# The first two weight blocks fetched in quarters, inputs and norm weights in order of need, and the sum of squares one chunk later

## The reference

```
x = x + 0.5 * swiglu(rms_norm(x, g1), w_gate, w_up, w_down)      # FFN, hidden width 2816
x = x + mixer(rms_norm(x, g2))                                   # attention and pooling
x = x + 0.5 * swiglu(rms_norm(x, g3), ...)
... # the second block: FFN, gated mixer, FFN, and a last rms_norm

def rms_norm(x, g):
    return x * rsqrt(mean(x * x, axis=-1) + 1e-6) * g
def swiglu(x, w_gate, w_up, w_down):
    return (silu(x @ w_gate) * (x @ w_up)) @ w_down
```

## Time and profile before

| | us |
|---|---|
| median of 3 runs | 1095.96 (1095.06 to 1097.74) |
| the profiled execution, its own time | 1094.97 |
| its span, from the first to the last instruction | 1093.2 |
| TensorE busy | 1080.8 (99% of the span) |
| VectorE busy | 783.8 (72%) |
| ScalarE busy | 617.4 (56%) |
| GpSimd busy | 187.8 (17%) |

### The profile page before, as it was taken

How to read it: one execution, slowest core, us unless ns; L and a number is a source line. 1 busy time by engine, 2 the same in 40 slices (tenths; PEclk the granted TensorE clock), 3 DMA queues, 4 the chain that set the end, 5 groups by cost and what they waited for, 6 DMA issues and landing times.

```text
span 1093.2 us, 17873 instructions
## 1 busy us (share of the span) xinstructions
PE 1080.8 (99%) x6282; PEld 944.2 (86%) x6282; DVE 783.8 (72%) x1114; ACT 617.4 (56%) x945; POOL 187.8 (17%) x199
## 2 busy tenths in 40 slices
PE   8999999999999999999999999999999999999997
PEld 6888888888988888888888888889988898888886
DVE  6866666797797666668666676787877669666664
ACT  7655544465675555456555545755655557555541
POOL 4411101020031111011111100133201012111100
PEclk9999999999999999999999999999999999999998
DMA  7755555453256555556555554655455545655561
GB/s 280 269 188 189 186 180 175 171 177 134 96 175 210 192 190 176 191 175 209 195 188 188 182 191 155 221 183 192 155 192 182 185 152 203 201 191 190 177 192 39
DMA packets 55571, 200.02 MB, mean 183 GB/s; under 512 B 6304, under 2 KB 6304, under 8 KB 55392
## 3 DMA queue, kind: packets, MB, share of 16 engines
q1 hardware_dynamic: 54576, 196.11, 52.9%
q0 software_dynamic: 512, 2.65, 0.6%
q10 hardware_dynamic: 432, 0.57, 0.2%
HBM read 198.26 MB, written 1.05 MB: 182 GB/s over the span
## 4 chain that ended last, share of the span: by engine, by line
PE 94%; DVE 4%; DMA 1%; ACT 0%; issue 0%; ACTq 0%; DVEq 0%
PE pair L1256 53%; PE pair L1257 27%; PE pair L1250 4%; PE pair L1252 4%; PE pair L1251 4%; DVE w_lo L780 1%; DVE x_hl L786 1%; PE pair L1472 1%; DMA x<-x_in 1%; PE pair L1482 0%; DVE x L797 0%; PE pair L1535 0%; PE pair L1577 0%; PE pair L1493 0%; DVE x_sq L926 0%
## 5 line engine op out<-in xcount | busy, mean ns | idle before, releaser
L780 DVE TENSOR_TENSOR w_lo<-w_raw,w_hi 128x1024 fp32r<-128x1024 f32 x369 | 462.1, 1259 | 226.3 <-ACT w_hi L429 225.9
L1256 PE MATMUL pair<-x_hl,w_hi 128*128 128x512 f32 x1728 | 606.6, 396 | 2.6 <-DVE x_hl L786 1.6
L429 ACT ACTIVATE w_hi<-w_raw 128x1024 fp32r<-128x1024 f32 x369 | 386.4, 1056 | 240.5 <-PE pair L1257 205.2
L1257 PE MATMUL pair<-x_hl,w_lo 128*128 128x256 f32 x1728 | 483.5, 280 | 0.0
L1256 PEld LDWEIGHTS pair<-x_hl,w_hi 128*128 128x128 f32 x1728 | 323.9, 187 | 80.5 <-DVE w_lo L780 2.0
L1257 PEld LDWEIGHTS pair<-x_hl,w_lo 128*128 128x128 f32 x1728 | 326.1, 189 | 0.1
L1256 PE MATMUL pair<-wide,w_hi 128*128 128x512 f32 x832 | 291.0, 394 | 0.0
L1257 PE MATMUL pair<-wide,w_lo 128*128 128x256 f32 x832 | 232.7, 280 | 0.0
L1256 PEld LDWEIGHTS pair<-wide,w_hi 128*128 128x128 f32 x832 | 156.0, 187 | 36.4
L1257 PEld LDWEIGHTS pair<-wide,w_lo 128*128 128x128 f32 x832 | 157.0, 189 | 0.0
L347 POOL TENSOR_TENSOR wide<-side,wide 128x256 fp32r<-128x256 f32 x88 | 86.5, 983 | 375.9 <-ACT wide L491 375.9
(11 more groups left out here) (185 smaller groups left out, 829.2 us busy)
## 6 DMA issues: line engine op xcount, KB each, us to landing
w_raw<-stream SPq DMA_DIRECT2D x369, 512.0 KB, 4.2
const<-const_in POOLq DMA_DIRECT2D x1, 1248.0 KB, 8.3
w_raw<-stream SPq DMA_DIRECT2D x4, 256.0 KB, 5.7
out<-x_sq SPq DMA_DIRECT2D x4, 256.0 KB, 2.6
rows<-rows_in POOLq DMA_DIRECT2D x1, 576.0 KB, 10.3
x<-x_in ACTq DMA_DIRECT2D x2, 256.0 KB, 5.7
x<-x_in SPq DMA_DIRECT2D x2, 256.0 KB, 7.0
sgu_w<-sgu_w_in POOLq DMA_DIRECT2D x1, 512.0 KB, 13.3
```

Source lines behind the costliest of these rows:

```text
L429: nc.scalar.activation(w_hi[:, slot, :], w_raw[:, slot, :], ACT.Copy).then_inc(w_hi_done, 1)
L780: nc.vector.tensor_tensor(w_lo[:, slot, :], w_raw[:, slot, :], w_hi[:, slot, :].bitcast(F32), ALU.subtract).then_inc(w_split, 1)
L1256: nc.tensor.matmul(dst, a_hi, b_hl.rearrange("p a s -> p (a s)"), start=first, stop=False, skip_group_check=True)
L1257: return nc.tensor.matmul(dst[:, 0:S], a_lo, b_hl[:, 0, :], start=False, stop=last, skip_group_check=True)
```

## The change

The left halves of blocks 0 and 1 become two quarters each, with transfers, copies, subtractions and waits of their own. Tile 0 and tile 1 of x become transfers of their own, with `cols` between them, and tiles 4 and 5 move from SP's queue to ACT's. On ACT, all squares move behind the split of block 2: tiles 0 to 3 ahead of the split of block 3, tiles 4 to 7 behind it. On TensorE the sum of squares of the first FFN moves from ahead of chunk 2 (blocks 4 and 5) to behind it; on ACT and DVE the splits of blocks 8 and 9 move from between the first steps of the FFN to ahead of the root and of its inverse. There are 12 warming matmuls in place of 16.

```diff
         @block.sync
-            for n in range(2):
-                sp.dma_start(w_raw[:, n, 0:HALF], stream[n, :, 0:HALF]).then_inc(half_arrived[n], 16)
+            for q in range(2):
+                for n in range(2):
+                    part = slice(q * QUARTER, (q + 1) * QUARTER)
+                    sp.dma_start(w_raw[:, n, part], stream[n, :, part]).then_inc(quarter_arrived[2 * q + n], 16)
             for n in range(2):
                 sp.dma_start(w_raw[:, n, HALF:BW], stream[n, :, HALF:BW]).then_inc(arrived[n], 16)
-            for c in range(2, 4):
-                sp.dma_start(x[:, 2 * c:2 * c + 2, :], x_in[:, 2 * c:2 * c + 2, :]).then_inc(x_loaded[c], 16)
+            sp.dma_start(x[:, 6:8, :], x_in[:, 6:8, :]).then_inc(x_loaded[2], 16)
...
+            def first_quarter(q):
+                for n in range(2):
+                    part = slice(q * QUARTER, (q + 1) * QUARTER)
+                    act.wait_ge(quarter_arrived[2 * q + n], 16)
+                    nc.scalar.activation(w_hi[:, n, part], w_raw[:, n, part], ACT.Copy).then_inc(quarter_hi_done, 1)
+
             def first_input():
-                for c in range(4):
-                    act.wait_ge(x_loaded[c], 16)
-                    input_hi(0, 2 * c)
-                    input_hi(0, 2 * c + 1)
-                    if c == 1:
-                        for n in range(2):
-                            act.wait_ge(arrived[n], 16)
-                            nc.scalar.activation(w_hi[:, n, HALF:BW], w_raw[:, n, HALF:BW], ACT.Copy).then_inc(w_hi_done, 1)
-                    if 1 <= c < 3:
-                        square(0, 2 * c - 2)
-                        square(0, 2 * c - 1)
+                first_quarter(0)
+                act.wait_ge(cols_loaded, 16)
+                for k in range(2):
+                    act.wait_ge(x_first[k], 16)
+                    input_hi(0, k)
+                first_quarter(1)
+                act.wait_ge(x_loaded[0], 16)
+                for k in range(2, 4):
+                    input_hi(0, k)
+                for n in range(2):
+                    act.wait_ge(arrived[n], 16)
+                    nc.scalar.activation(w_hi[:, n, HALF:BW], w_raw[:, n, HALF:BW], ACT.Copy).then_inc(w_hi_done, 1)
+                for c in range(2, 4):
+                    act.wait_ge(x_loaded[c - 1], 16)
+                    for k in range(2 * c, 2 * c + 2):
+                        input_hi(0, k)
                 split(2)
+                for k in range(4):
+                    square(0, k)
+                split(3)
                 for k in range(4, KC):
                     square(0, k)
...
             def ffn(e, n0, p):
-                for b in range(3, 8):
+                for b in range(3 if p else 4, 8 if p else 10):
                     split(n0 + b)
                 rms_root(p)
...
                 fetch(0, 2)
-                split(n0 + 8)
+                if p:
+                    split(n0 + 8)
                 gate(0)
                 fetch(1, 3)
                 hidden(0)
-                split(n0 + 9)
+                if p:
+                    split(n0 + 9)
                 gate(1)
...
-            act.dma_start(x[:, 0:2, :], x_in[:, 0:2, :]).then_inc(x_loaded[0], 16)
+            act.dma_start(x[:, 0, :], x_in[:, 0, :]).then_inc(x_first[0], 16)
             act.dma_start(cols[:], cols_in).then_inc(cols_loaded, 16)
-            act.dma_start(x[:, 2:4, :], x_in[:, 2:4, :]).then_inc(x_loaded[1], 16)
+            act.dma_start(x[:, 1, :], x_in[:, 1, :]).then_inc(x_first[1], 16)
+            act.dma_start(x[:, 2:4, :], x_in[:, 2:4, :]).then_inc(x_loaded[0], 16)
+            act.dma_start(x[:, 4:6, :], x_in[:, 4:6, :]).then_inc(x_loaded[1], 16)
...
         @block.vector
...
-                for b in range(3, 7):
+                for b in range(3, 7 if p else 9):
                     split(n0 + b)
                 mean_square(p)
-                split(n0 + 7)
+                split(n0 + (7 if p else 9))
                 inverse_root(p)
...
         @block.tensor
...
             def ffn(e, n0, p):
-                if p == 0:
-                    pe.wait_ge(half_split, 2)
                 for k in range(KC):
+                    if p == 0 and k in (0, 2):
+                        pe.wait_ge(quarter_split, k + 2)
...
-                sum_squares(p)
+                if p:
+                    sum_squares(p)
...
                     chunk(f, (f + 2) % 4)
+                    if p == 0 and f == 2:
+                        sum_squares(p)
...
-WARM = 16
+WARM = 12
```

More of the change, by code:

```diff
@@ L45 @@
 BW = 1024
-HALF = BW // 2
+HALF, QUARTER = BW // 2, BW // 4
 RING = 4
@@ L181, in build @@
         arrived = [sem(f"arrived{i}") for i in range(RING)]
-        half_arrived = [sem(f"half_arrived{i}") for i in range(2)]
-        half_hi_done = sem("half_hi_done")
-        half_split = sem("half_split")
+        quarter_arrived = [sem(f"quarter_arrived{i}") for i in range(4)]
+        quarter_hi_done = sem("quarter_hi_done")
+        quarter_split = sem("quarter_split")
         w_hi_done = sem("w_hi_done")
@@ L187, in build @@
         w_used = sem("w_used")
-        x_loaded = [sem(f"x_loaded{c}") for c in range(4)]
+        x_first = [sem(f"x_first{k}") for k in range(2)]
+        x_loaded = [sem(f"x_loaded{c}") for c in range(1, 4)]
         cols_loaded = sem("cols_loaded")
@@ L1208, in gated_mixer @@
                 residual(p)
[L1210 to L1215, removed]
+            for q in range(2):
+                for n in range(2):
+                    part = slice(q * QUARTER, (q + 1) * QUARTER)
+                    dve.wait_ge(quarter_hi_done, 2 * q + n + 1)
+                    nc.vector.tensor_tensor(w_lo[:, n, part], w_raw[:, n, part], w_hi[:, n, part].bitcast(F32),
+                                            ALU.subtract).then_inc(quarter_split, 1)
+                for k in range(2 * q, 2 * q + 2):
+                    input_lo(0, k)
             for n in range(2):
```

## The result

The changed kernel is slower: median 1098.6 us of 22 runs (1095.26 to 1103.12), against 1094.57 us for the kernel before in 22 runs of the same series. The two medians are 4.0 us apart; the ratio formed from all the runs is 1.0046 [1.0035, 1.0057], or 5.0 us. Its profiled execution took 1100.22 us with a span of 1098.4 us, 5.2 us more than the execution of the earlier trace rows.

What follows compares the result with a forecast made beforehand. TensorE's unbroken stream bounds the kernel. Block 2's 1.2 us gain is spent on the late sum and root, and GpSimd's 1.6 us delay less 0.75 us spare makes +0.9 us: 1096.9 us, range 1093.8 to 1099.4 us.

Steps and rivals of the forecast that it cites:

- The wait at block 8: TensorE waits briefly at block 8 for the first add, due 6.95 us behind block 5's end; block 8 0.9 us late.
- Step 1: Front of TensorE's stream: with squares moved, ACT copies block 2 sooner and block 2 starts at 14.2 us, 1.2 us earlier.
- Step 2: GpSimd's queue: the seven additions start at about 13.6 us, take 8.2 us again and end at 21.8 us, 1.6 us later.
- rival E: Port lock between VectorE and GpSimd: additions take 10.0 us, block 11 starts 2.7 us later; 1098.7 us, chance 0.05.
- Step 3: Block 11 on TensorE: late hidden_lo delays DVE's subtraction, so block 11 starts at 42.27 us, 0.9 us later than before.
- the clock as a rival: At the start: twelve warming matmuls may end before the clock rises, leaving early blocks at 1.2 GHz; block 11 3.2 us later.
- the prediction's last sign of being wrong: On TensorE: the prediction is wrong if a matmul pair takes 0.64 us after 8 us.
- A: A gain arrives: block 2 gains 1.5 us, only the 0.8 us stall is lost; 0.7 us faster, 1095.3 us, chance 0.25.
- B: Small transfers are slow: block 2 gains only 0.5 us, block 11 starts 1.6 to 2.3 us later; 1098 us, chance 0.10.
- D: First sum of squares stalls TensorE beyond 0.8 us because DVE is still at block 8; 1097.5 to 1098 us, chance 0.04.
- slower: Outcome that the measurement tells the changed kernel from no change, 0.3% (3.3 us), on the slow side; chance 0.06.
- C: Clock still at 1.2 GHz for blocks 0 and 1 after fewer warming matmuls: 3.2 us later, 1099.2 us, chance 0.06.

Runs made afterwards that it cites:

- experiment 1: Changed kernel with GpSimd's tables moved behind hidden_lo(0) in its queue: median 1096.69 us, ratio 1.0029.
- experiment 3: Changed kernel with the last four of GpSimd's seven additions of squares 8 columns wide instead of 256: median 1096.83 us, ratio 1.0031.
- experiment 5: Kernel before with only the squares moved, tiles 0 to 3 behind block 2's split, 4 to 7 behind block 3's: 1099.05 us, ratio 1.004.
- experiment 6: Changed kernel with the sum of squares and the splits of blocks 8 and 9 back at their old places: 1099.01 us, ratio 1.0043.
- experiment 12: Changed kernel, unchanged, profiled a second time: one time of 1099.37 us, no interval.
- experiment 8: Changed kernel with the squares alone back between the inputs, the sum of squares still one chunk later: 1100.13 us, ratio 1.0062.
- experiment 10: Changed kernel with the squares back between the inputs and the split of block 9 behind the inverse root: 1096.89 us, ratio 1.002.
- experiment 7: Kernel before with only the quarters, the input order and 12 warming matmuls: 1094.46 us, ratio 1.0011.
- experiment 4: Changed kernel with ten matmuls on zeros ahead of block 11, to fill the pause: median 1098.77 us, ratio 1.0052.
- experiment 9: Changed kernel with GpSimd's tables behind hidden_lo(0) and the split of block 9 behind the inverse root: 1095.7 us, ratio 1.0019.
- experiment 11: Kernel before, unchanged, profiled a second time: one time of 1092.0 us, no interval.
- experiment 2: Kernel before with GpSimd's tables moved behind hidden_lo(0): 1094.76 us, ratio 1.0001.

## Why the prediction was wrong

**What held.** The places were right: a wait with `ms` (0.65 against 0.8 us), one at block 10, one at block 11 released by DVE's subtraction, with DVE behind `hidden_lo`. With E, the end of block 5, at 26.50 us, the first `add` ended at E + 6.94, where 6.95 had been worked out, block 10 came at E + 13.3 (13.1), and the time from the last addition to `hidden_lo` was 17.4 us (17.6 before). The wait at block 8 did not come: the 6.95 us were met, but so was block 8's place, moved by the wait with `ms`. From 52 us on there is no difference.

**Step 1, "block 2 1.2 us earlier": 0.2 us.** The sentence that failed is that the 5.66 us of blocks 0 and 1 "fit in front of block 2 either way, if their last tiles come by 12.8 us". Tiles 4 to 7 are 8 pairs, 2.83 us; for block 2 at 14.2 us tile 4 has to start by 11.4 us. It started at 12.30, released by DVE's input half, because ACT's inputs of tiles 4 to 7 stood behind the right half of block 1, which landed at 10.4 us. TensorE's own tile 4 had run at about the same time before; when I took away ACT's squares, that became what set block 2. DVE had block 2's split ready at 14.84 us.

**Step 2, GpSimd's queue, +1.6 us: +4.65 us.** It is two terms. The additions began at 14.27 instead of 13.6 us, since ACT's copy of block 2 was at 12.53 and not 11.8. And they took 10.6 us, not the 8.2 carried over from before. That size was the worst error, and rival E (10.0 us, 0.05) had it nearly right. The additions one by one, start to end in us, worked out from the trace:

```
before  11.00-11.72 12.10-13.00 13.14-13.88 14.46-15.94 16.08-16.81 16.96-18.49 18.63-20.17
after   14.27-15.44 15.59-16.33 16.47-18.00 18.15-19.80 19.94-21.47 21.62-23.15 23.29-24.82
```

Alone an addition takes 0.74 us, beside a subtraction of DVE 1.53 us. Before, four of seven ran beside nothing or nearly so; behind the splits of blocks 2 and 3 DVE always has a subtraction at hand, and only one was that short. The argument against E was that the first addition had taken 0.72 us; it does not count, because the change moves the additions out of that very place. DVE's subtractions pay too: four of the six among them take 1.4 to 1.8 us instead of 1.23. The Trainium skill (SBUF — State Buffer, section SBUF: two separate sides) calls the shared port pair "an exclusive lock, not a bandwidth split"; these rows agree, with 0.74 us for an addition alone and 1.53 us beside a subtraction. No experiment here moves the subtractions, so that they lengthen the additions is read from the rows alone.

**Step 3, block 11, +0.9 us: +3.7 us.** This follows from step 2: 4.4 us later at DVE, less 0.75 us to spare. Experiments 1 and 3 show it from two sides.

**The missing step, the clock behind the pause: +1.6 us.** I had the clock as a rival at the program's start only. It did not happen there: the trace has the granted clock rise at 4.78 us, among the twelve warming matmuls, whose weight loads start every 0.42 us up to there and every 0.21 us behind it, and from 6.33 us on pairs take 0.35 us. It fell behind the pause at block 11, where a pair takes 0.64 us (45.98 to 46.62 us), so the prediction's last sign of being wrong did show, but at 46 us and not at the start. The Trainium skill (TensorE: Matmul & The Clock Gate, section The HAM clock gate) has the low clock as the default, to which an idle engine returns; these rows show it after 2.2 us without work. In experiments 5 and 6 it came behind waits of about 3 us, in experiment 12 behind 1.93 us, in experiment 8 behind 1.93 and 1.79 us, and not behind waits of 1.5 and 1.6 us (experiment 10). Nor did it come behind one of 1.78 us in experiment 7, so the length of the pause alone does not decide.

**Rivals.** A failed with step 1. B was wrong as a cause (experiment 7: no cost of the quarters and the order shows), although tile 4 does not come sooner with them either. D did not occur in the changed kernel, where the wait with `ms` was 0.65 us; it is what made that wait 1.5 us in experiment 10. The sum of +0.9 us stands against 5.2 us between the spans and 5.0 us by the ratio. That the forecast time of 1096.9 us is only 1.7 us below the measured median is luck: the median of the kernel before is 1.4 us lower in this series than the one I started from, which hides part of the error. The chance of "slower" (0.06) was set from single mechanisms (E with 2.7 us, C with 3.2), while here two terms added up and a third, the clock, stood on them.

**What stays open.** How much of the median's 5 us the low clock is, since experiment 4's median did not fall. In the 22 runs of the changed kernel, the 16 with a mean clock of 0.995 or less have a median of 1099.4 us and the other six 1098.4, a difference that the pace alone could make. Open too is what the late sum of squares costs at best: experiments 1 and 3 leave some 1.3 us, experiment 9 0.5 us, each with an interval that starts close to 1.

## What to carry over

Before a step is moved on one engine, list what runs beside it at its new place: an operation's duration belongs to its neighbours, and an addition on GpSimd that cost 0.74 us beside an idle VectorE cost 1.53 us beside a busy one. A gain at the front is worth what the next-latest supplier leaves of it; compute for each supplier the time by which it must deliver, with the work that still follows. And price a pause of TensorE of about 2 us and more with its echo: here the 1.2 GHz stretch behind it added 1.6 us to 2.2 us of waiting.

## Unexpected: two paces of one matmul pair

The kernel before had three runs of 1095 to 1098 us when I made the prediction. Its 90 runs in the series of the experiments fall into clusters near 1091.2, 1094.5 and 1097.7 us (32, 43 and 15 runs). Behind the start, its two profiles differ in one thing. The stretch of the first FFN in the execution of the earlier trace rows:

```profile
50.00:190.00 140.00, 140.00 (x794) 121.31 (x793) 93.63 (x123) 74.97 (x111) 20.77 (x22) 1.00 0.55 188
```

and in that of experiment 11:

```profile
50.00:190.00 140.00, 140.00 (x810) 122.39 (x809) 95.91 (x125) 75.69 (x113) 20.82 (x22) 1.00 0.58 193
```

TensorE is busy throughout and the granted clock is 1.00 in both, yet one makes 794 matmuls and the other 810: 0.3527 against 0.3457 us for a pair, by the counts. One pace holds for a whole FFN and changes only from one to the next (in experiment 6 the second FFN has the longer one, in experiments 2 and 8 the last), and is worth about 3 us for each FFN. Kernels of both kinds show both, so it says nothing about the change; but it moves a single execution by as much as the change does, which is why the spans above are compared at equal pace. For experiment 6, with two FFNs at the longer pace, the span of 1101.1 us less an estimated 2.7 is 5.2 us over before. What sets the pace I have not found.
